# Latent attention: the squares of two heads folded onto 64 rows each, one sum product for both, and the first two score blocks made in one visit

## The reference

```python
def mla_layer(x, positions, norm_g, w_in, q_norm_g, kv_norm_g, w_uq, w_ukv, qn_g, kn_g, w_out):
    u = rms_norm(x, norm_g) @ w_in
    cq, ckv, kpe, z = jnp.split(u, [Q_LORA, Q_LORA + KV_LORA, Q_LORA + KV_LORA + QK_ROPE], axis=-1)
    q = (rms_norm(cq, q_norm_g) @ w_uq).reshape(B, S, C_HEADS, QK_HEAD)
    kv = (rms_norm(ckv, kv_norm_g) @ w_ukv).reshape(B, S, C_HEADS, QK_NOPE + V_HEAD)
    k_nope, v = jnp.split(kv, [QK_NOPE], axis=-1)
    k = jnp.concatenate([k_nope, jnp.broadcast_to(kpe[:, :, None, :], (B, S, C_HEADS, QK_ROPE))], axis=-1)
    q = rms_norm(q, qn_g)
    k = rms_norm(k, kn_g)
    ...   # rope on the last 64 columns of q and k
    o = block_causal_attention(q, k, v).reshape(B, S, C_WIDTH) * jax.nn.silu(z)
    return x + o @ w_out

def block_causal_attention(q, k, v):
    ...
    for qb in range(S // Q_BLOCK):            # 4 blocks of 128 queries
        s = jnp.einsum('bqhd,bkhd->bhqk', q[:, q0:q1], k[:, :q1]) * scale
        mask = chunk_id[q0:q1, None] >= chunk_id[None, :q1]     # chunks of 64
        p = jax.nn.softmax(jnp.where(mask, s, -jnp.inf), axis=-1)
        outs.append(jnp.einsum('bhqk,bkhd->bqhd', p, v[:, :q1]))
```

## Time and profile before

| what | us |
|---|---|
| median of 3 executions | 2619.42 (2616.99 to 2619.45) |
| the profiled execution | 2617.52 |
| its span, first to last instruction | 2615.7 |
| PE busy | 2600.1 (99%) |
| DVE busy | 1417.8 (54%) |
| ACT busy | 1023.4 (39%) |
| POOL busy | 233.7 (9%) |
| granted TensorE clock, mean | 1.000 |

### The profile page before, as it was taken

The page is one execution under the profiler, slowest core; times in us unless marked ns, Lnnn a source line. Parts: engine busy times, 40 slices in busy tenths (PEclk is TensorE's granted clock), DMA queues, the critical chain, the costliest instruction groups (busy, mean ns, idle before and its releaser), DMA issues.

```text
span 2615.7 us, 33036 instructions
## 1 busy us (share of the span) xinstructions
PE 2600.1 (99%) x12326; PEld 2122.3 (81%) x12326; DVE 1417.8 (54%) x1863; ACT 1023.4 (39%) x1592; POOL 233.7 (9%) x172
## 2 busy tenths in 40 slices
PE   8999999999999999999999999999999999999999
PEld 7888887878888888888887778888887888888877
DVE  5444248875444335444258765444236657845773
ACT  4222135654222223222136653222235554334663
POOL 0000024201000010000034101000001110012210
PEclk9999999999999999999999999999999999999999
DMA  4222233113222223222232112222222222322221
GB/s 165 96 96 96 96 99 103 65 41 105 96 96 96 96 81 112 96 96 96 96 112 90 57 62 93 96 97 96 97 95 73 81 89 85 105 97 93 85 71 55
DMA packets 70323, 239.13 MB, mean 91 GB/s; under 512 B 8528, under 2 KB 10832, under 8 KB 70224
## 3 DMA queue, kind: packets, MB, share of 16 engines
q1 hardware_dynamic: 69792, 236.91, 26.6%
q10 hardware_dynamic: 432, 0.87, 0.1%
HBM read 230.15 MB, written 2.10 MB: 89 GB/s over the span
## 4 chain that ended last, share of the span: by engine, by line
PE 93%; DVE 3%; issue 2%; ACT 1%; DVEq 1%; POOL 0%; POOLq 0%; DMA 0%; ACTq 0%; SPq 0%
PE bank L419 20%; PE bank L421 20%; PE bank L420 20%; PE score L419 5%; PE score L420 5%; PE score L421 5%; PE flip_bank L419 2%; PE flip_bank L421 2%; PE flip_bank L420 2%; PE score L1182 1%; PE flip_bank L1210 1%; PE bank L2768 1%; PE score L2736 1%; PE score L1923 1%; PE bank L1232 1%
## 5 line engine op out<-in xcount | busy, mean ns | idle before, releaser
L393 DVE TENSOR_TENSOR w_lo<-w_raw,w_hi 128x1024 fp32r<-128x1024 f32 x425 | 526.2, 1240 | 538.4 <-ACT w_hi L353 527.3
L419 PE MATMUL bank<-h_hi,w_hi 128*128 128x512 f32 x1840 | 733.4, 399 | 1.1 <-DVE w_lo L393 1.1
L421 PE MATMUL bank<-h_hi,w_lo 128*128 128x512 f32 x1840 | 717.4, 390 | 0.0
L420 PE MATMUL bank<-h_lo,w_hi 128*128 128x512 f32 x1840 | 716.4, 389 | 0.0
L353 ACT ACTIVATE w_hi<-w_raw 128x1024 fp32r<-128x1024 f32 x427 | 447.5, 1051 | 383.6 <-DMA w_raw<-stream 383.0
L419 PEld LDWEIGHTS bank<-h_hi,w_hi 128*128 128x128 f32 x1840 | 345.7, 188 | 75.3 <-issue 5.0
L421 PEld LDWEIGHTS bank<-h_hi,w_lo 128*128 128x128 f32 x1840 | 345.4, 188 | 73.2
L420 PEld LDWEIGHTS bank<-h_lo,w_hi 128*128 128x128 f32 x1840 | 346.0, 188 | 70.8 <-issue 2.4
L553 ACT ACTIVATE hid_hi<-tmp 128x512 f32 (+1 forms) x88 | 55.6, 632 | 408.1 <-DVE tmp L778 408.1
L772 DVE TENSOR_TENSOR tmp<-bank,rstd 128x512 f32<-128x512 f32 x132 | 91.1, 691 | 148.3 <-PE bank L421 148.0
L548 ACT ACTIVATE tmp<-tmp 128x512 f32<-128x512 f32 x88 | 55.6, 632 | 248.7 <-DVE tmp L772 248.7
(11 more groups left out here) (535 smaller groups left out, 3832.8 us busy)
## 6 DMA issues: line engine op xcount, KB each, us to landing
w_raw<-stream SPq DMA_DIRECT2D x427, 512.0 KB, 3.2
tmp<-tmp SPq DMA_DIRECT2D x64, 64.0 KB, 2.0
x_tok<-x SPq DMA_DIRECT2D x4, 512.0 KB, 6.8
wx_raw<-stream SPq DMA_DIRECT2D x4, 512.0 KB, 4.5
out<-out_tok SPq DMA_DIRECT2D x8, 256.0 KB, 2.0
tmp<-qr SPq DMA_DIRECT2D x16, 64.0 KB, 2.6
tab_in_f<-tables SPq DMA_DIRECT2D x1, 704.0 KB, 10.4
cos_sin<-rope ACTq DMA_DIRECT2D x1, 512.0 KB, 4.9
```

The costliest lines, as they stand in the source:

```text
L393: nc.vector.tensor_tensor(w_lo[:, s, :], w_raw[:, s, :], w_hi[:, s, :].bitcast(F32), ALU.subtract).then_inc(lo_ready, 1)
L419: nc.tensor.matmul(dst, whi, xhi, start=start, stop=False)
L420: nc.tensor.matmul(dst, whi, xlo, start=False, stop=False)
L421: return nc.tensor.matmul(dst, wlo, xhi, start=False, stop=stop)
```

## The change

Four edits in the latent attention layer.

1. The squares of the two `ckv` tiles are added on POOL first (new, L2200), and PE sums one tile instead of two.
2. Queries: ACT writes each head's square in two halves of 64 rows (L2256, L2257). The half that lies on the head's own rows (0 to 63 for head 0, 64 to 127 for head 1) goes to `q_sq[own, 0]`, the other half is moved over to the same rows of `q_sq[own, 1]`. POOL adds the two 128-row tiles and then the rope squares (L2222, L2224), and now waits for both heads. PE has both heads' values in one 128-row tile, and four matmuls against a two-column table (`halves`, ones on rows 0 to 63 and on rows 64 to 127) give both heads' sums (L2722). The visit stands after one dense tile of the `z` unit, or after five of them for pair 0.
3. Keys: the same folding (L2281, L2282). POOL does four operations per pair instead of six. PE sums each head over its own 64 rows (L2731, L2733), upper parts of both heads first, then the lower parts. For pair 0 both stand behind `z` 0.
4. Scores: at b = 0 PE makes the scores of blocks 0 and 1 in one visit; block 0 lies in columns 0 to 127 of each head's bank, block 1 in 128 to 383. At b = 1 `scores` returns at once.

```diff
         def _(pool):
+            pool.wait_ge(ckv_in, KVT)
+            nc.gpsimd.tensor_tensor(ckv_sq[:, 0, :], ckv_sq[:, 0, :], ckv_sq[:, 1, :], ALU.add).then_inc(kv_added, 1)
...
             def key_squares(u):
-                for j in range(2):
-                    pool.wait_ge(k_evac, 2 * u + j + 1)
-                    nc.gpsimd.tensor_tensor(k_sq[0:HEAD, j, :], k_sq[0:HEAD, j, :], kpe_sq[0:HEAD, :], ALU.add)
-                    pool.drain()
-                    nc.gpsimd.tensor_copy(k_sq_hi[k_at(u)][:, j, :], k_sq[:, j, :])
-                    pool.drain()
-                    nc.gpsimd.tensor_tensor(k_sq_lo[:, j, :], k_sq[:, j, :], k_sq_hi[k_at(u)][:, j, :].bitcast(F32),
-                                            ALU.subtract).then_inc(k_split, 1)
+                pool.wait_ge(k_evac, 2 * u + 2)
+                nc.gpsimd.tensor_tensor(k_sq[:, 0, :], k_sq[:, 0, :], k_sq[:, 1, :], ALU.add)
+                pool.drain()
+                nc.gpsimd.tensor_tensor(k_sq[:, 0, :], k_sq[:, 0, :], kpe_sq[:, :], ALU.add)
+                pool.drain()
+                nc.gpsimd.tensor_copy(k_sq_hi[k_at(u)][:, 0, :], k_sq[:, 0, :])
+                pool.drain()
+                nc.gpsimd.tensor_tensor(k_sq_lo[:, 0, :], k_sq[:, 0, :], k_sq_hi[k_at(u)][:, 0, :].bitcast(F32),
+                                        ALU.subtract).then_inc(k_split, 1)
 
             def query_squares(u):
...
-                for j in range(2):
-                    pool.wait_ge(q_evac, 2 * u + j + 1)
-                    rows = slice(HEAD * j, HEAD * j + HEAD)
-                    ins = nc.gpsimd.tensor_tensor(q_sq[rows, j, :], q_sq[rows, j, :], rope_sq[rows, u % 2, :], ALU.add)
-                ins.then_inc(q_added, 1)
+                pool.wait_ge(q_evac, 2 * u + 2)
+                nc.gpsimd.tensor_tensor(q_sq[:, 0, :], q_sq[:, 0, :], q_sq[:, 1, :], ALU.add)
+                pool.drain()
+                nc.gpsimd.tensor_tensor(q_sq[:, 0, :], q_sq[:, 0, :], rope_sq[:, u % 2, :], ALU.add).then_inc(q_added, 1)
...
                     src = c_bank("k", 2 * u + j)[:, :]
-                    nc.scalar.activation(k_sq[:, j, :], src, ACT.Square)
+                    own, other = slice(HEAD * j, HEAD * j + HEAD), slice(HEAD - HEAD * j, P - HEAD * j)
+                    nc.scalar.activation(k_sq[own, 0, :], src[own, :], ACT.Square)
+                    nc.scalar.activation(k_sq[own, 1, :], src[other, :], ACT.Square)
                     nc.scalar.activation(kn[:, u % 2, j, :], src, ACT.Copy, scale=col("kn_nope")).then_inc(k_evac, 1)
...
-                    ins = column(dst, TB + b, b, ckv_sq[:, 0, :], ckv_sq[:, 1, :])
+                    ins = column(dst, TB + b, b, ckv_sq[:, 0, :])
...
+            def query_sums(u):
+                dst = fresh("qsum", u)
+                pe.wait_ge(q_added, u + 2)
                 for b in range(TB):
-                    ins = column(dst, TB * j + b, b, q_sq[:, j, :])
...
+                    ins = nc.tensor.matmul(dst[:, 2 * b:2 * b + 2], q_sq[:, 0, P * b:P * b + P], table("halves", 2),
+                                           start=True, stop=True)
+                ins.then_inc(q_summed, 1)
+
+            def key_sums(u):
+                dst = [fresh("ksum", 2 * u + j) for j in range(2)]
+                pe.wait_ge(k_split, u + 1)
+                rows = [slice(HEAD * j, HEAD * j + HEAD) for j in range(2)]
+                for j in range(2):
+                    nc.tensor.matmul(dst[j][:, :], ones_r[rows[j], :], k_sq_hi[k_at(u)][rows[j], 0, :], start=True, stop=False)
+                for j in range(2):
+                    nc.tensor.matmul(dst[j][:, :], ones_r[rows[j], :], k_sq_lo[rows[j], 0, :], start=False,
+                                     stop=True).then_inc(k_summed, 1)
...
             def scores(k):
                 u, b = C_STEPS[k]
-                width = P * (b + 1)
+                if b == 1:
+                    return
+                blocks = (0, 1) if b == 0 else (b,)
...
                 for j in range(2):
-                    nc.tensor.matmul(score[:, j, 0:width], qn[:, u % 2, j, P * b:P * b + P], kn[:, u % 2, j, 0:width],
-                                     start=True, stop=False)
+                    for e in blocks:
+                        nc.tensor.matmul(score[:, j, score_cols(e)], qn[:, u % 2, j, P * e:P * e + P],
+                                         kn[:, u % 2, j, 0:P * (e + 1)], start=e == blocks[0], stop=False)
+                for e in blocks:
+                    for j in range(2):
+                        rows = slice(HEAD * j, HEAD * j + HEAD)
+                        nc.tensor.matmul(score[:, j, score_cols(e)], qr[rows, u, P * e:P * e + P],
+                                         kr[rows, u % 2, 0:P * (e + 1)], start=False, stop=False)
...
                 if (kind, t) == ("z", 1):
-                    dense("z", 1, 0, 4)
-                    query_sums(0, 0)
-                    dense("z", 1, 4, 5)
-                    query_sums(0, 1)
+                    dense("z", 1, 0, 5)
+                    query_sums(0)
                     dense("z", 1, 5, KT)
```

More of the change, by code:

```diff
@@ L2251, in queries @@
                     src = c_bank("q", 2 * u + j)[:, :]
-                    nc.scalar.activation(q_sq[:, j, :], src, ACT.Square)
+                    own, other = slice(HEAD * j, HEAD * j + HEAD), slice(HEAD - HEAD * j, P - HEAD * j)
+                    nc.scalar.activation(q_sq[own, 0, :], src[own, :], ACT.Square)
+                    nc.scalar.activation(q_sq[own, 1, :], src[other, :], ACT.Square)
                     nc.scalar.activation(qn[:, u % 2, j, :], src, ACT.Copy, scale=col("qn_nope")).then_inc(q_evac, 1)
@@ L2305, in exps @@
                 for j in range(2):
-                    ins = nc.scalar.activation(c_probs[:, k % 2, j, 0:width], score[:, j, 0:width], ACT.Exp,
+                    ins = nc.scalar.activation(c_probs[:, k % 2, j, 0:width], score[:, j, score_cols(b)], ACT.Exp,
                                                scale=q_inv(u)[:, j, b:b + 1], bias=softstat[:, 2 * k + j, 0:1],
@@ L2493, in maxima @@
                 dve.wait_ge(c_scored, k + 1)
-                nc.vector.tensor_reduce(softstat[:, 2 * k:2 * k + 2, 0], score[:, :, 0:P * (b + 1)], AX_X, ALU.max,
+                nc.vector.tensor_reduce(softstat[:, 2 * k:2 * k + 2, 0], score[:, :, score_cols(b)], AX_X, ALU.max,
                                         negate=True)
@@ L2709, in latent_sums @@
                 ins.then_inc(lat_summed, 1)
-            def query_sums(u, j):
-                dst = c_bank("qsum", u) if j else fresh("qsum", u)
-                if j == 0:
-                    pe.wait_ge(q_added, u + 2)
+            def query_sums(u):
+                dst = fresh("qsum", u)
+                pe.wait_ge(q_added, u + 2)
                 for b in range(TB):
-                    ins = column(dst, TB * j + b, b, q_sq[:, j, :])
-                if j == 1:
-                    ins.then_inc(q_summed, 1)
-            def key_sum(u, j):
-                dst = fresh("ksum", 2 * u + j)
-                pe.wait_ge(k_split, 2 * u + j + 1)
-                nc.tensor.matmul(dst[:, :], ones_r[:, :], k_sq_hi[k_at(u)][:, j, :], start=True, stop=False)
-                nc.tensor.matmul(dst[:, :], ones_r[:, :], k_sq_lo[:, j, :], start=False, stop=True).then_inc(k_summed, 1)
+                    ins = nc.tensor.matmul(dst[:, 2 * b:2 * b + 2], q_sq[:, 0, P * b:P * b + P], table("halves", 2),
[10 more added lines that the diff above has]
+                                     stop=True).then_inc(k_summed, 1)
             def scores(k):
                 u, b = C_STEPS[k]
-                width = P * (b + 1)
+                if b == 1:
+                    return
+                blocks = (0, 1) if b == 0 else (b,)
                 if b == 0:
@@ L2735, in scores @@
                 for j in range(2):
-                    nc.tensor.matmul(score[:, j, 0:width], qn[:, u % 2, j, P * b:P * b + P], kn[:, u % 2, j, 0:width],
-                                     start=True, stop=False)
-                for j in range(2):
-                    rows = slice(HEAD * j, HEAD * j + HEAD)
-                    nc.tensor.matmul(score[:, j, 0:width], qr[rows, u, P * b:P * b + P], kr[rows, u % 2, 0:width],
-                                     start=False, stop=False)
-                for j in range(2):
-                    ins = nc.tensor.matmul(score[:, j, P * b:width], table_b("identity"), table_b("chunked"), start=False,
-                                           stop=True)
-                ins.then_inc(c_scored, 1)
+                    for e in blocks:
[6 more added lines that the diff above has]
+                                         kr[rows, u % 2, 0:P * (e + 1)], start=False, stop=False)
+                for j in range(2):
+                    for e in blocks:
+                        end = score_cols(e).stop
+                        ins = nc.tensor.matmul(score[:, j, end - P:end], table_b("identity"), table_b("chunked"),
```

(8 more changed lines are left out.)

13 lines of the change are left out of this document (6 added, 7 removed).

## The result

| | us |
|---|---|
| kernel before, median of 16 executions | 2617.89 (2616.83 to 2619.83) |
| changed kernel, median of 16 executions | 2622.44 (2620.7 to 2625.37) |
| ratio, 95% interval | 1.0018 (1.0011 to 1.0025) |
| span of the profiled execution, before and after | 2615.7, 2620.5 |
| PE busy, before and after | 2600.1, 2597.0 |

The change makes the kernel slower by 4.5 us, just under what I had called measurable, but the interval is clear of 1. I had forecast 1.3 us faster, 2618.1, with a range up to 2621.2. The base of that forecast was the median of three executions, 2619.42; over 16 the kernel before is at 2617.89. The changed kernel's times are also spread wider than those of before.

What follows compares the result with a forecast made beforehand. PE, busy 99% of the span, was taken as the bound. Savings of -6.4 us plus waits of +1.1 and +4.0 gave -1.3, so 2618.1 from a median of 2619.42; range 2614.2 to 2621.2.

Steps and rivals of the forecast that it cites:

- latent squares: PE's sums of the ckv squares: four columns go at 0.23 us each, -0.9; the POOL addition costed at nothing.
- query sums: PE's query sums: eight records fewer per pair, -3.5 us over four pairs, and -0.1 for one visit fewer at pair 0.
- key sums: PE's key sums as two pairs of 64-row matmuls: -0.2 us over four pairs, and -0.3 for pair 0's old wait.
- merged scores: One score visit for blocks 0 and 1 enters and leaves 64-row mode once: -1.4 us over four pairs.
- the rival of serial pairs: Key sums' 64-row matmuls run one after another: +1.2 us instead of -0.2, 2619.5 in all; chance 0.07.
- the full gain: ACT comes in time and neither new PE wait appears: -6.4 us, 2613.0; chance 0.09.
- the 0.35: Saving per pair from the merged score visit, taken from a range of 0.30 to 0.38 us.
- the value waits: Second half of the values, pairs 1 to 3: PE waits 1.3 us each for ACT's first key copy, +4.0.
- hence 0.48 in a queue: ACT's 64x512 half square: 0.48 us to the next start, priced from rows of 8x512 and 128x512.
- My slower rival: Moved half squares on ACT cost more than 0.48 us, delaying key copies of pairs 1 to 3; 2625.3 at 0.6; chance 0.05.
- its x: Extra cost of each half square over 0.48 us; PE pays 12x, and from 0.54 the result is over +5.2.
- the wait at the query sums: Query sums of pair 0: PE waits 1.1 to 1.8 us for POOL in place of 0.4, +1.1.

Runs made afterwards that it cites:

- p_stay: Changed kernel without the folding; the other half's square is written on the rows it is read from; one execution, 2621.65 us.
- p_cols: Changed kernel without the folding; each head's square cut by columns (2 x 128x256) instead of rows; one execution, 2616.27 us.
- x_wait2: Kernel before with only the query sums of pair 0 two dense tiles earlier; median 2622.08 us, ratio 1.0014.
- a_q7: Changed kernel with the query sums of pair 0 after seven dense tiles of z 1 instead of five; median 2619.22 us, ratio 1.0003.
- e_keys_old: Changed kernel with the keys' squares and sums as before (one full square per head, 128-row sums); median 2620.16 us, ratio 1.0008.
- e_key_first: Changed kernel; at b = 1 ACT takes the first key head's squares and copy ahead of the weight cut and exponentials; 2620.72 us, ratio 1.0009.
- e_nomerge: Changed kernel without the merged score visit, scores of blocks 0 and 1 made separately as before; median 2619.01 us, ratio 1.0002.
- x_wait1: Kernel before with only the query sums of pair 0 three dense tiles earlier; median 2622.32 us, ratio 1.0016.
- e_cs: Kernel before with only the latent squares added on POOL and the merged score visit; median 2617.6 us, ratio 0.9996.

## Why the prediction was wrong

The savings were right almost to the tenth: latent squares -0.9, query sums -3.4 for -3.6, key sums -0.5, merged scores -1.1 over three pairs. The merged visit lasts 2.46 (2.45 forecast). The key sums' two pairs are 0.33 to 0.34 apart, side by side: the rival of serial pairs is out, and so is the full gain. At pair 3 the 0.35 did not come, since a wait of 0.4 for `w_lo` stood behind it, which every kernel with merged scores has.

The mechanism of the waits was right too, and where they stand. The term of the sum that failed is the value waits, +4.0 where +5.6 was measured, and the step behind it is the price of a half square, "hence 0.48 in a queue": 0.60 was measured wherever the neighbour begins on another partition. I had the duration from two rows and took the overlap of 128-row neighbours for granted. On the way to the first key copy the second query head cost ACT 1.80 instead of my 1.54, and the key head 1.89 to the copy's end instead of 1.65: 0.5 in all. The three waits are 1.65 on average instead of 1.3. My slower rival was near this: it made the moved half squares dear, while `p_stay` shows the long distance without a move, and its x is 0.12 to 0.16, far from the 0.54 from which it alone would have decided. No run takes x alone away; `p_cols` shortens the halves as well. The same price delays the key copies of pair 0, where the sum of cq takes a value bank: +0.6, a place I had not looked at.

Between the forecast and the profiled pair, -1.3 and +3.6, lie 4.9 us: 1.6 in the value waits, 1.6 at half clock, about 0.65 at the merged scores of pair 3, 0.6 at the sum of cq, 0.3 in the wait at the query sums and 0.2 in their saving.

What the prediction did not have at all is the lower clock. I priced each wait at its length. `x_wait2` shows 3.7 us for 1.3 of added wait, and `a_q7` 3.2 for 1.4 taken away. Over the executions, what comes with the wait at the query sums is about 1.8 of the 4.5 us, and it is part of the spread. `a_q7` has all three value waits and the lower clock in only one of eleven executions, so they cost little more than their length there. What they add once PE has waited at the query sums stays open: the changed kernel's profile has the stretch behind one of them and none behind the query sums. Nor is it shown what decides whether a given wait brings it; the profiles of `e_keys_old` and `e_key_first` have a wait of 1.8 at the query sums and no half clock.

The upper end of the range, 2621.2, took in waits of up to 1.6 by their length, and nothing for what follows a wait on an engine that had none before. Without the 1.8 us the changed kernel would be at about 2620.6, inside it, but that is luck of the base: the range ended 1.8 above the 2619.42 it was laid on, and 2620.6 is 2.7 above the 2617.89 measured since. So the dearer half squares and the two places that I had put at nothing or as a gain (the sum of cq, `w_lo` at pair 3) carry the profiled pair to +2.0 without the half clock, already past the range's +1.8.

## What to carry to other kernels

Where TensorE is never idle, a new wait can cost more than its length, because the lower clock can follow. At one place here it was two to three times the length (3.7 for 1.3, 3.2 for 1.4); at three others, in `a_q7`, little more than the length. So put the dearer price into the range, look at the mean granted clock of every execution and not of one profile alone, and take the wait away by putting the consumer later if that can be done. Before work is split into smaller instructions for another engine's sake, look at start-to-start distances of neighbours of exactly that shape and partition offset; durations alone hide the overlap that is lost. And count the copies that free a bank: each instruction added ahead of one is paid wherever the bank's next user stands.

## What the runs showed of the hardware

- ACT instructions reading PSUM overlap their neighbour by about 0.1 us (0.48 between starts for 0.60 of duration) when both begin on the same partition. Where one begins on partition 64 and the next on 0, or the other way round, on the side read or the side written, the distance is 0.60; behind the scaled copy it is 0.71 instead of 0.57 (changed kernel and `p_stay`; no other offset was tried).
- In the profiles TensorE's granted clock went to 0.50 for 3.4 to 6.8 us behind waits of 1.1 to 2.4 at the query sums (`p_cols`, `x_wait2`, `e_nomerge`, `p_stay`, `x_wait1`), once behind a wait of 0.36 between dense matmuls and two single-column visits (`e_cs`), and once behind one of three value waits of 1.5 to 1.8 (changed kernel). It began 0.3 to 2.4 us after the wait had ended, so it can stand in the trace behind dense matmuls and not at the idle time. Two further profiles with a wait of 1.8 at the query sums have no such stretch.
